# Cross-layer keys and values as three fp32r products of split rows and weights

## What is computed

```python
def nsa_shared_kv(h, kv_norm, w_kv, cmp_pos, cmp_w1, cmp_w2):
    hn = rms_norm(h, kv_norm)
    kv = (hn @ w_kv).reshape(b, s, 3, 2, NSA_KV_GROUPS, HEAD_DIM)     # 512 x 1024 @ 1024 x 1536
    blk = kv[:, :, 0][:, idx]                                         # 31 overlapping blocks of 32 tokens
    blk = blk + cmp_pos                                               # (broadcast)
    hid = jax.nn.gelu(jnp.einsum('bncgf,cfe->bncge', blk, cmp_w1))
    cmp = jnp.einsum('bncge,ced->bncgd', hid, cmp_w2)
    k_cmp, v_cmp = cmp[:, :, 0], cmp[:, :, 1]
    k_slc, v_slc = partial_rope(kv[:, :, 1, 0]), kv[:, :, 1, 1]
    k_win, v_win = partial_rope(kv[:, :, 2, 0]), kv[:, :, 2, 1]
```

## Time and profile before

| | |
|---|---|
| median of 3 runs | 2587.71 us (2584.94 to 2590.36) |
| the profiled execution | 2586.47 us |
| its span | 2584.7 us, so 1.77 us lie outside it |
| mean granted TensorE clock | 0.973 of full speed |
| busy: TensorE, VectorE, GpSimd, ScalarE | 93%, 53%, 41%, 38% of the span |
| key and value projections on TensorE | 674.69 to 762.30 us |
| first product of the queries | 786.43 us |

### The profile page before, as it was taken

One profiled execution on the slowest core, in us unless ns is written; L12 is line 12 of the kernel. 1 busy time (PEld: TensorE's weight loads), 2 busy tenths in 40 slices (PEclk: granted clock), 3 DMA queues, 4 the chain that ended last, 5 costly groups with the idle time before them and its releaser, 6 DMA issues.

```text
span 2584.7 us, 37305 instructions
## 1 busy us (share of the span) xinstructions
PE 2413.4 (93%) x14005; PEld 1919.4 (74%) x14005; DVE 1368.6 (53%) x2006; ACT 987.6 (38%) x1828; POOL 1049.7 (41%) x977
## 2 busy tenths in 40 slices
PE   7999899999999898999999899989989899899995
PEld 6777788888576666888887788869978797555553
DVE  4334255335364785534534665661167643688885
ACT  3344322222211674322224243332155401277775
POOL 7554444444006005444444644526841276411111
PEclk9999999999999999999999899989999899899998
DMA  4111233333232000333331211112211022499996
GB/s 134 58 50 58 82 106 98 98 89 106 65 106 90 1 2 25 107 97 98 98 98 33 77 42 42 43 49 74 84 31 34 25 90 83 139 322 361 366 368 229
DMA packets 267876, 268.63 MB, mean 104 GB/s; under 512 B 13339, under 2 KB 198518, under 8 KB 267750
## 3 DMA queue, kind: packets, MB, share of 16 engines
q1 hardware_dynamic: 262998, 253.91, 30.5%
q0 software_dynamic: 4752, 12.98, 2.0%
HBM read 256.10 MB, written 10.75 MB: 103 GB/s over the span
## 4 chain that ended last, share of the span: by engine, by line
PE 79%; DVE 8%; DMA 5%; ACT 3%; issue 2%; POOL 1%; SPq 0%; DVEq 0%; ACTq 0%; POOLq 0%
PE psum L2766 16%; PE psum L2769 16%; PE psum L2770 16%; DMA ex_tile<-in_w_down 3%; PE psum L1520 3%; PE psum L2404 2%; PE psum L2470 2%; PE psum L852 2%; PE psum L1234 2%; PE psum L854 2%; PE psum L853 2%; PE psum L1297 1%; PE psum L1289 1%; PE psum L2276 1%; DMA ex_tile<-in_w_gate 1%
## 5 line engine op out<-in xcount | busy, mean ns | idle before, releaser
L2766 PE MATMUL psum<-x_hi,w_hi 128*128 128x264 f32 (+2 forms) x1560 | 528.7, 339 | 20.1 <-DVE k_lo L1758 8.1
L2769 PE MATMUL psum<-x_lo,w_hi 128*128 128x264 f32 (+2 forms) x1560 | 518.5, 332 | 0.0
L2846 POOL TENSOR_TENSOR w_lo<-ring_tile,w_hi 128x1024 fp32r<-128x1024 f32 x128 | 308.0, 2407 | 370.7 <-ACT w_hi L2829 368.4
L804 POOL TENSOR_TENSOR w_hi<-ring_tile,one 128x256 fp32r<-128x256 f32 (+1 forms) x284 | 235.8, 856 | 480.8 <-PE psum L2770 449.3
L2770 PE MATMUL psum<-x_hi,ring_tile_lo 128*128 128x264 f32 (+2 forms) x1096 | 341.4, 311 | 0.0
L2766 PEld LDWEIGHTS psum<-x_hi,w_hi 128*128 128x128 f32 x1560 | 297.3, 191 | 55.2 <-issue 21.9
L2769 PEld LDWEIGHTS psum<-x_lo,w_hi 128*128 128x128 f32 x1560 | 297.5, 191 | 27.8 <-issue 1.5
L808 POOL TENSOR_TENSOR ring_tile_lo<-ring_tile,w_hi 128x256 fp32r<-128x256 f32 (+1 forms) x284 | 294.3, 1063 | 8.2
L3077 DVE TENSOR_TENSOR h<-psum,h 128x512 f32<-128x512 f32 x80 | 55.0, 691 | 337.3 <-PE psum L2770 270.1
L2829 ACT ACTIVATE w_hi<-ring_tile 128x1024 fp32r<-128x1024 f32 x128 | 134.9, 1057 | 251.7 <-PE psum L2770 240.9
L2770 PEld LDWEIGHTS psum<-x_hi,ring_tile_lo 128*128 128x128 f32 x1096 | 208.6, 190 | 11.2
(11 more groups left out here) (428 smaller groups left out, 5187.4 us busy)
## 6 DMA issues: line engine op xcount, KB each, us to landing
ring_tile<-in_mlp_w SPq DMA_DIRECT2D x128, 512.0 KB, 4.0
ex_tile<-in_w_gate SPq DMA_DIRECT2D x64, 512.0 KB, 12.4
ex_tile<-in_w_up SPq DMA_DIRECT2D x64, 512.0 KB, 11.9
ex_tile<-in_w_down SPq DMA_DIRECT2D x64, 512.0 KB, 12.0
ring_tile<-in_w_in SPq DMA_DIRECT2D x52, 512.0 KB, 3.8
ring_tile<-in_sb_w_qkv SPq DMA_DIRECT2D x24, 512.0 KB, 3.8
ring_tile<-in_nsa_w_kv SPq DMA_DIRECT2D x12, 512.0 KB, 3.8
ring_tile<-in_sb_w_o SPq DMA_DIRECT2D x8, 512.0 KB, 3.7
```

Source lines behind the costliest of these rows:

```text
L804: last = pool.tensor_tensor(hi[:, cols], raw[:, cols], one[:, :].broadcast_to([P, D // len(parts)]), ALU.mult)
L2766: upper = pe.matmul(dst, a_hi, b_hi, start=first, stop=False)
L2769: pe.matmul(dst, a_hi, b_lo, start=False, stop=False)
L2846: pool.tensor_tensor(lo, raw, hi.bitcast(F32), ALU.subtract).then_inc(split_w, 1)
```

## The change

The projections become split products. Norm 2 is now one of those that split: ScalarE writes `kx_hi`, VectorE writes `kx_lo` in the place of `xT`. ScalarE writes the upper part of each weight tile to one of two buffers (`kv_upper`), the one of tile n as soon as tile n-2 is done, and GpSimd writes the lower part over the raw tile in the ring, in four pieces (`kv_pool`). The eight transposed tiles become 8 times 3 products of 512 columns (tile 0 in two halves of 256). Of the value tiles a pair is loaded together: one slot holds half of the rows of both, and `values` adds 48 products of 256 columns for each slot, the rows now being the stationary operand.

`kx_hi` lies where `k_lo` will be. So all 16 instructions for `k_lo` now come after tile 11, behind the value copies and the blocks of the second half, and before the GELU. `k_raw` has four buffers instead of two and lies where the gates' transpose is written, so that `gates_act` also waits for `cmp_hh` 1. ScalarE's list is interleaved anew. The diff, without address moves of no consequence:

```diff
-        k_raw = at("k_raw", [P, 2, SEQ], STAGE_AT + 99904)
-        k_turn = at("k_turn", [P, 2, SEQ], STAGE_AT + 104000)
...
+        k_raw = at("k_raw", [P, 4, SEQ], XN_AT)
+        kw_hi = at("kw_hi", [P, SPLITS2, D], STAGE_AT + 95872, F32R)
+        kx_hi = at("kx_hi", [P, KT, SEQ], STAGE_AT + 16384, F32R)
+        kx_lo = at("kx_lo", [P, KT, L2], XT_AT, F32R)
+        k_turn = at("k_turn", [P, 2, SEQ], STAGE_AT + 104064)
...
+        KV_VALUES = (6, 7, 10, 11)
+
+        def kv_tile(n):
+            if n in KV_VALUES:
+                first = n - n % 2
+                return rows_tiles(A["nsa_w_kv"], lambda t: n % 2 * (KT // 2), lambda t: first * P, 2 * P)
+            return cols_tile(A["nsa_w_kv"], lambda t: n)
...
-            ring.load(sp, "kv_first", [cols_tile(A["nsa_w_kv"], lambda t, j=j: j) for j in range(RING)])
+            ring.load(sp, "kv_first", [kv_tile(n) for n in range(RING)])
...
-            ring.load(sp, "kv_last", [cols_tile(A["nsa_w_kv"], lambda t, j=j: j) for j in range(RING, 12)])
+            ring.load(sp, "kv_last", [kv_tile(n) for n in range(RING, 12)])
...
+                if u == 2 and s == QT:
+                    kv_upper(act, 0)
                 if s >= 2 and u in SPLIT_NORMS:
                     split_x_act(act, u, s - 2)
-                if s >= 2 and u == 2:
+                if u == 2 and s in (2, 3):
                     raw_x_act(act, s - 2)
+            if u == 2:
+                kv_upper(act, 1)
+                raw_x_act(act, 2)
+                raw_x_act(act, 3)
...
-        SPLIT_NORMS = (0, 1, 3, 4, 6)
+        SPLIT_NORMS = (0, 1, 2, 3, 4, 6)
...
-            return {6: (x2_hi, x2_lo), 3: (x3_hi, x3_lo)}.get(u, (x_hi, x_lo))
+            return {6: (x2_hi, x2_lo), 3: (x3_hi, x3_lo), 2: (kx_hi, kx_lo)}.get(u, (x_hi, x_lo))
...
-        SPLIT_COUNTS = (("sb", 3 * PAIRS), ("sb_o", KT), ("nsa", NSA_PAIRS), ("nsa_o", KT), ("df", 3 * HEADS2), ("br0", BR_SPLITS),
+        SPLIT_COUNTS = (("sb", 3 * PAIRS), ("sb_o", KT), ("kv", 12), ("nsa", NSA_PAIRS), ("nsa_o", KT), ("df", 3 * HEADS2), ("br0", BR_SPLITS),
...
+            hi, lo = split_of(u)
...
-                last = mm3_K(pe, dst[:, cols], w, x_hi[:, :, cols], x_lo[:, :, cols])
+                last = mm3_K(pe, dst[:, cols], w, hi[:, :, cols], lo[:, :, cols])
...
+        def kv_raw(eng, n):
+            return ring.wait(eng, "kv_first", n) if n < RING else ring.wait(eng, "kv_last", n - RING)
+
+        def kv_slot(n):
+            return (ring.plan["kv_first"][n] if n < RING else ring.plan["kv_last"][n - RING])[0]
+
+        def kv_upper(act, n):
+            raw = kv_raw(act, n)
+            if n >= SPLITS2:
+                act.wait_ge(kv_mm, n - SPLITS2 + 1)
+            act.activation(kw_hi[:, n % SPLITS2, :], raw, ACT.Copy).then_inc(split2_hi, 1)
+
+        def kv_pool(pool):
+            for n in range(12):
+                raw = kv_raw(pool, n)
+                pool.wait_ge(split2_hi, SPLIT_BASE["kv"] + n + 1)
+                for c in range(4):
+                    cols = slice(D // 4 * c, D // 4 * (c + 1))
+                    last = pool.tensor_tensor(ring_lo[:, kv_slot(n), cols], raw[:, cols], kw_hi[:, n % SPLITS2, cols].bitcast(F32), ALU.subtract)
+                last.then_inc(split2, 1)
+
         def kv_pe(pe):
+            def values(n, w):
+                hi, lo = (x.rearrange("p (k n) -> p k n", n=2 * P) for x in w)
+                upper = n % 2
+                for t in range(QT):
+                    dst = bank[2 + t // 2][:, t % 2 * 2 * P:(t % 2 + 1) * 2 * P]
+                    for k in range(KT // 2):
+                        rows = slice(t * P, (t + 1) * P)
+                        a_hi, a_lo = (x[:, upper * (KT // 2) + k, rows] for x in (kx_hi, kx_lo))
+                        first = pe.matmul(dst, a_hi, hi[:, k, :], start=(upper == 0 and k == 0 and t % 2 == 0), stop=False, skip_group_check=True)
+                        if t == 0 and k == 0:
+                            first.then_inc(slot_free, 1)
+                        pe.matmul(dst, a_lo, hi[:, k, :], start=False, stop=False, skip_group_check=True)
+                        last = pe.matmul(dst, a_hi, lo[:, k, :], start=False, stop=(upper == 1 and k == KT // 2 - 1), skip_group_check=True)
+                return last
+
             def tile(n):
-                slot = ring.wait(pe, "kv_first", n) if n < RING else ring.wait(pe, "kv_last", n - RING)
+                pe.wait_ge(split2, SPLIT_BASE["kv"] + n + 1)
+                w = (kw_hi[:, n % SPLITS2, :], ring_lo[:, kv_slot(n), :])
                 if n >= 4:
-                    pe.wait_ge(kv_ev, n - 3)
-
-                begun = slot_free if n else None
-                if n in (6, 7, 10, 11):
-                    for t in range(QT):
-                        last = mm_N(pe, bank[n % 4][:, t * P:(t + 1) * P], slot, t, begun=begun if t == 0 else None)
+                    pe.wait_ge(kv_ev, n - (2 if n in (6, 10) else 3))
+                if n in KV_VALUES:
+                    last = values(n, w)
                 else:
-                    last = mm_T(pe, bank[n % 4][:, :], slot, xT[:, :, 0:SEQ], begun=begun)
+                    w = [x.rearrange("p (k n) -> p k n", n=P) for x in w]
+                    if n:
+                        last = mm3_K(pe, bank[n % 4][:, :], w, kx_hi, kx_lo[:, :, 0:SEQ], begun=slot_free)
+                    else:
+                        last = first_product(pe, 2, bank[0], w)
...
-                pe.matmul(bank[4 + n % 2][:, :], rot1[:, :], k_raw[:, n % 2, :], start=True, stop=True).then_inc(kv_rot, 1)
+                pe.matmul(bank[4 + n % 2][:, :], rot1[:, :], k_raw[:, KV_ROT[n], :], start=True, stop=True).then_inc(kv_rot, 1)
...
-                    dve.tensor_copy(k_raw[:, n % 2, :], bank[n % 4][:, :]).then_inc(kv_ev, 1)
+                    dve.tensor_copy(k_raw[:, KV_ROT[n], :], bank[n % 4][:, :]).then_inc(kv_ev, 1)
                 for n in (n0, n0 + 1):
-                    raw = k_raw[:, n % 2, :]
+                    raw = k_raw[:, KV_ROT[n], :]
                     dve.wait_ge(kv_rot, KV_ROT[n] + 1)
                     dve_t.inc(dve.tensor_tensor(k_turn[:, 0, :], raw, cos1[:, :], ALU.mult))
                     step(dve, dve.tensor_tensor(k_turn[:, 1, :], bank[4 + n % 2][:, :], sin1[:, :], ALU.mult))
                     dve.tensor_tensor(raw, k_turn[:, 0, :], k_turn[:, 1, :], ALU.add).then_inc(kv_k, 1)
                     dve.wait_ge(kv_k, KV_ROT[n] + 1)
-                    dve.wait_ge(kv_mm, n + 3)
-                    dve.tensor_copy(v_all[:, br, :, 2 * (n - n0):2 * (n - n0) + 2, :],
-                                    bank[(n + 2) % 4][:, :].rearrange("p (t g d) -> p t g d", t=QT, g=2)).then_inc(kv_ev, 1)
+                for n in (n0, n0 + 1):
+                    dve.wait_ge(kv_mm, n0 + 4)
+                    dve.tensor_copy(v_all[:, br, 2 * (n - n0):2 * (n - n0) + 2, :, :],
+                                    bank[2 + n - n0][:, :].rearrange("p (t g d) -> p t g d", t=2, g=GROUPS)).then_inc(kv_ev, 1)
+                if br == 0:
+                    own_x_lower_dve(dve, range(KT))
+                take_blocks(br, 0, CMP_KT)
+
+            for br, n0 in ((0, 4), (1, 8)):
+                for n in (n0, n0 + 1):
                     dve.wait_ge(kv_h, KV_ROT[n] + 1)
                     for hi, src in key_halves(n, br, n0):
                         lo = k_lo[hi[0], hi[1], br, :]
                         last = dve.tensor_tensor(lo, src, k_hi[hi[0], hi[1], br, :].bitcast(F32), ALU.subtract)
                     step(dve, last)
-                if br == 0:
-                    own_x_lower_dve(dve, range(KT))
-                take_blocks(br, 0, CMP_KT)
...
         def kv_act(act):
-            own_x_act(act)
-            for br, n0 in ((0, 4), (1, 8)):
+            def keys_upper(br, n0):
                 for n in (n0, n0 + 1):
                     act.wait_ge(kv_k, KV_ROT[n] + 1)
                     for hi, src in key_halves(n, br, n0):
                         last = act.activation(k_hi[hi[0], hi[1], br, :], src, ACT.Copy)
                     last.then_inc(kv_h, 1)
+
+            for n in range(2, 6):
+                kv_upper(act, n)
+            own_x_act(act, range(KT // 2))
+            kv_upper(act, 6)
+            own_x_act(act, range(KT // 2, KT))
+            for n in (7, 8):
+                kv_upper(act, n)
+            keys_upper(0, 4)
+            for n in (9, 10, 11):
+                kv_upper(act, n)
+            keys_upper(1, 8)
...
+            act.wait_ge(cmp_hh, 1)
...
-        def own_x_act(act):
-            for k in range(KT):
+        def own_x_act(act, ks):
+            for k in ks:
...
                     flow_pool(pool, 2)
+                    kv_pool(pool)
                     queries_pool(pool)
```

More of the change, by code:

```diff
@@ L271, in build_program @@
         cmp_h = at("cmp_h", [P, 2, 2, GROUPS * N_CMP], STAGE_AT + 97920)
-        k_raw = at("k_raw", [P, 2, SEQ], STAGE_AT + 99904)
-        k_turn = at("k_turn", [P, 2, SEQ], STAGE_AT + 104000)
```

(13 more changed lines are left out.)

## The result

| | before | after |
|---|---|---|
| median | 2586.63 us (2584.41 to 2590.36) | 2596.61 us (2594.93 to 2598.32) |
| ratio to before, 95% interval | | 1.004 [1.003, 1.0051] |
| profiled execution, its span | 2586.47, 2584.7 us | 2594.93, 2593.1 us |

A forecast was written before the change was run, and what follows sets the result against it. The prediction took TensorE, busy for 93% of the span, as the bound. Its terms, -16.3 + 4.6 + 4.5 + 8.5 + 3.8 = +5.1 us on 2586.47, gave 2591.6, written as 2592, range 2581 to 2599.

The forecast's parts named there:

- bound of 0.2%: Whole kernel: 5.2 us counts as a difference, so slower is above 2592.9 us and faster below 2582.5.
- The three places: The parts of the stage where the prediction expected the change to act: start, products and tail.
- products: TensorE's 12 projection tiles and 4 rotations: 71.3 us instead of 87.6, a gain of 16.3 us.
- start: Ahead of the first tile: ScalarE's longer list and GpSimd's pieces make TensorE start 4.6 us later (bounds +3.9, +5.1).
- rotation of tile 8: After tile 7: VectorE's list, slowed beside GpSimd, makes TensorE wait 4.5 us for this rotation (bounds 0 and 6).
- tail: After the last projection tile: `k_lo` beside GpSimd, then GELU on VectorE, delay the queries by 8.5 us (bounds +3.9, +13).
- clock: TensorE's clock may fall at three gaps, 1.8 us each, weighted by chance: +3.8 us (bounds 0 and 5.4).
- the third rival: Value products with weights of their own stay at f32 pace, 4 x 1.4 us missing: 2597 us; chance 0.05.
- Splits: ScalarE's and GpSimd's weight splits keep up: at most 5.2 us per tile, inside the 5.56 of the previous tile.
- The rival with +13: The VectorE-GpSimd lock costs a full piece each time: tail +13, rotation 6, total 2598 to 2599 us; chance 0.15.
- The first rival: The splits hinder each other little: rotation wait 0.3, tail +3.9, total -5.5 us, 2582 us; chance 0.25.
- the last rival: The tail is not late, since something lets VectorE take `k_lo` before the last projection tile ends: 2577 us; chance 0.05.

The follow-up runs named there:

- e5: Changed kernel with ScalarE's upper part of weight tile 0 one step sooner, ahead of the last row tile's scaling; ratio to before 1.0042.
- e9: Changed kernel with the edits of e1, e2 and e5 together, and without TensorE's wait for the last `xT` ahead of the first product; ratio to before 0.9951.
- e3: Changed kernel with GpSimd starting to split the query weights only after VectorE's first GELU; ratio to before 1.0006.
- e4: Changed kernel plus 32 unused products of 512 columns in TensorE's gap ahead of the second compression layer; ratio to before 1.0028.
- e2: Changed kernel with VectorE's copy of tile 8's product moved ahead of the 16 block instructions; ratio to before 1.0020.
- e1: Changed kernel with twelve of the 16 `k_lo` instructions moved behind the GELU, and another address for `gates_T`; 2581.91 us, ratio to before 0.9987.
- e6: Changed kernel plus twelve unused identity products behind the transposes of each of the second, third and fourth row tiles; ratio to before 1.0043.
- e10: e9 plus twelve unused identity products behind the transposes of each of the second and third row tiles; 2572.54 us, ratio to before 0.9943.

## Why the prediction was right

The time lay inside the range. By the prediction's own bound of 0.2% the kernel is slower, which had 0.41, as much as "same". The three places and what ends the wait in each were confirmed; the sum was not. The range is 18 us wide and holds the kernel before as well, so that being inside it says little. The stage is 5.3 us longer than the sum has it, while the profiled execution lies 3.3 above the 2591.6 of the sum, because the rest of the kernel happened to be 1.9 us shorter than in the execution of before. By its own terms:

| term | predicted | measured |
|---|---|---|
| products | -16.3 | -16.3 |
| start | +4.6 | +4.6 |
| rotation of tile 8 | +4.5 | +4.1 |
| wait for GpSimd's split of tile 9 | 0 | +0.5 |
| tail | +8.5 | +10.2 |
| clock | +3.8 | +7.3 |
| sum, stage | +5.1 | +10.4 |

- *Products.* From 678.45 to 758.17 are 79.7 us; less the gap (4.1), the wait (0.5) and the slow clock of tiles 0 and 10 (3.8) leave 71.3, as predicted. A transposed tile took 5.53, a value tile 5.66. That value products with weights of their own stay at the f32 pace, the third rival, is ruled out.
- *Start.* Counted in the stage, 12.2 us to the first product where before takes 7.6. ScalarE's list took 7.85 us from the first split on, where the steps of the prediction add up to 7.9, and GpSimd's pieces took 3.25 instead of 3.5. e5 and e9 show that a second wait lies right behind this one.
- *Rotation.* VectorE's two items were both mis-sized, in opposite directions: `x_lo` 8.1 (6.4 predicted), blocks 5.9 (6.9). I had four of GpSimd's pieces against `x_lo` and six against the blocks. The splits of tiles 9 and 10 ran from 728.64 to 733.36 and from 734.18 to 738.11, so that six of the eight `x_lo` met one, at 0.54 each where I had 0.37 (3.2 instead of 1.5), and four pieces were left for the blocks (2.0 instead of 3). That the gap came out within 0.4 us of the forecast is luck: in e3 and e4, the same code up to there, the blocks take 7.0 and the gap is 5.15. e2 shows that this list was the cause of the gap.
- *Splits.* "5.2 us for the chain, still inside" failed at one tile: beside `x_lo` GpSimd's four pieces took 4.72 instead of 4.0, and TensorE waited half a microsecond.
- *Tail.* The `k_lo` term was right: 16.0 us measured, 15.8 predicted (T + 21.1 for both). The GELU took 4.93 and 5.02 and not 4.18 each: in the execution before, two of its instructions on VectorE were not held up (0.42 and 0.29 us where after has 0.99 and 0.71). e1 shows the order as the cause; e3 shows that without the contention most of it goes, 7.7 us from T to the queries. The rival with +13 is ruled out for quarter pieces: `k_lo` took 1.0 us and not over 1.2.
- *Clock.* This is the step that failed in size: 7.3 us, above even the upper bound of 5.4. I gave the start and the rotation a chance to keep the clock, and counted 1.8 us at most for each fall. The clock fell in all three. Tile 0 lost 2.0, rotation and tile 10 lost 1.8, the second compression layer with its copies 1.3, the queries 2.2 (52.3 us against 50.0). The tail's is checked by e4 (3.6) and the start's by e6 (tile 0 back to 5.9). I had counted one loss for the gap of the tail, but two pieces of work stand behind it, the small second layer and then the queries, with a short wait between, and both ran slow. The Trainium skill's rule ("TensorE: Matmul & The Clock Gate", Why this matters for your kernels) would have put all three gaps in, and was right here against my reading of the earlier trace rows: the gap ahead of the stage kept its clock before with 8 us of scattered transposes, but not with 12.

The first rival (the splits hinder each other little) is ruled out by 1.0 for each `k_lo`, though e3 shows what it would have been worth. Against the last rival I held that nothing in the code lets VectorE take `k_lo` before T. That is true, and was the wrong question: most of `k_lo` could as well come after the GELU, and e1 took 13.7 us off.

## What to carry to other kernels

When a change moves the work of a fast engine to helpers, list for each helper what it does between the two points where the fast engine waits for it, in program order, and put first what is waited for: three edits of order alone turned +10 us into -10 here. Count each new gap of TensorE twice, for its length and for the clock of everything behind it, small steps included. And before a step of 1 us is explained, look at how much executions of the same code differ at that place: here it was 1.2 us, and a rule drawn from e6 without that look did not hold.

## What the runs showed of the hardware

- The stage's first gap held 32 transposes in both kernels. Before, with 7.6 us to the first product, the clock stayed at 1.00; after, with 12.2, it was at 0.59 from 672 to 674 and at 0.50 from 674. With 36 or 24 products of the identity added there, 128 columns each, it stayed at 1.00 over the whole gap (e6, e10).
- Two-input instructions of VectorE (`x_lo`, 128x512) take 0.68 us alone, 1.22 beside GpSimd's 256-column pieces, and 0.68 or up to 2.89 beside 1024-column ones; the total is nearly the same (8.1 and 9.3 us for eight).
- Scaling blocks of 128x124 slow down too: 16 take 3.9 us alone and 5.9 to 7.0 beside GpSimd's splits in four executions of the same code (after, e1, e3, e4). In after four of them took about 0.8 us instead of 0.3.
